# Expert layer: 49 of 128 hidden blocks made beside the choice of experts and the gates, 80 of 256 sums ranked, one-hot rows by wide comparisons

## The reference

```python
q = (h @ wq).reshape(B, S, PEER_HEADS, 2, PEER_QDIM // 2)
sub_scores = jnp.einsum('bshpk,hpnk->bshpn', q, subkeys)
top_v, top_i = lax.top_k(sub_scores, PEER_TOPK)                       # 16 of 128, twice for each of 8 heads
cand = (top_v[..., 0, :, None] + top_v[..., 1, None, :]).reshape(B, S, PEER_HEADS, 256)
cand_i = (top_i[..., 0, :, None] * N_KEYS + top_i[..., 1, None, :])
best_v, best_pos = lax.top_k(cand, PEER_TOPK)                         # 16 of 256 sums
expert = jnp.take_along_axis(cand_i, best_pos, axis=-1)
gates = jax.nn.softmax(best_v, axis=-1)
...
ub = jnp.take(u, eb, axis=0)
hid = jax.nn.gelu(jnp.einsum('tkd,td->tk', ub, xb)) * gb
vb = jnp.take(v, eb, axis=0)
return jnp.einsum('tk,tkd->td', hid, vb)
```

## Time and profile before

| | us |
|---|---|
| median of 3 runs | 3894.51 (3891.09 to 3894.8) |
| the profiled execution | 3889.89 |
| its span, first to last instruction | 3888.1 |
| DVE's last step of query to first keys | 590 to 628 |
| one-hot stage | 628 to 837 |
| start of dense | 837 to 864 |
| dense | 864 to 1922 |
| all that follows | 1922 to 3888 |

### The profile page before, as it was taken

How to read it: one execution, slowest core, us unless ns; L and a number is a source line. 1 busy time by engine, 2 the same in 40 slices (tenths; PEclk the granted TensorE clock), 3 DMA queues, 4 the chain that set the end, 5 groups by cost and what they waited for, 6 DMA issues and landing times.

```text
span 3888.1 us, 40982 instructions
## 1 busy us (share of the span) xinstructions
PE 3479.1 (89%) x16313; PEld 2824.5 (73%) x16313; DVE 2080.8 (54%) x3469; ACT 1499.7 (39%) x2428; POOL 766.2 (20%) x646
## 2 busy tenths in 40 slices
PE   5897993669999999999999997899898799899998
PEld 3466572659999999999878885678776474477887
DVE  2445599967666666666555524544532322344332
ACT  1222124965555555555532224345441111223222
POOL 0000104955444444444300000000000000000000
PEclk9895996879999999999989998999896598799999
DMA  4430511258777777777445522122121032032322
GB/s 170 131 114 1 201 49 44 125 209 303 278 277 278 273 274 274 274 281 280 142 152 184 185 81 82 68 82 68 58 91 37 0 102 83 6 98 83 96 98 76
DMA packets 175567, 554.74 MB, mean 143 GB/s; under 512 B 14801, under 2 KB 66385, under 8 KB 156945
## 3 DMA queue, kind: packets, MB, share of 16 engines
q1 hardware_dynamic: 138048, 350.52, 26.2%
q0 software_dynamic: 37328, 201.61, 14.5%
HBM read 514.06 MB, written 38.01 MB: 142 GB/s over the span
## 4 chain that ended last, share of the span: by engine, by line
PE 80%; DVE 14%; ACT 3%; DMA 2%; issue 1%; SPq 0%; DVEq 0%; ACTq 0%
PE ps L228 10%; PE ps L230 10%; PE ps L229 10%; PE ps L237 5%; PE ps L1329 4%; PE ps L1330 4%; PE ps L1315 4%; PE ps L1313 4%; PE ps L1314 4%; PE ps L1328 4%; DVE peerg_OH L1152 2%; PE ps L312 2%; PE ps L168 1%; PE ps L2033 1%; PE ps L2032 1%; PE ps L509 1%
## 5 line engine op out<-in xcount | busy, mean ns | idle before, releaser
L220 DVE TENSOR_TENSOR Wl<-W,Wh 128x1024 fp32r<-128x1024 f32 x363 | 438.1, 1207 | 716.1 <-ACT Wh L214 716.1
L214 ACT ACTIVATE Wh<-W 128x1024 fp32r<-128x1024 f32 x363 | 377.1, 1039 | 605.9 <-PE ps L230 570.0
L1292 POOL TENSOR_TENSOR peer_Y<-peer_Y,peerv_UV 128x1024 f32<-128x1024 f32 x128 | 380.2, 2970 | 531.6 <-ACT peerv_UV L1353 531.6
L1313 PE MATMUL ps<-peer_Hh,Wh 128*128 128x384 f32 x1024 | 344.8, 337 | 5.2 <-DVE Wl L220 5.2
L1315 PE MATMUL ps<-peer_Hh,Wl 128*128 128x384 f32 x1024 | 344.8, 337 | 0.0
L1314 PE MATMUL ps<-peer_Hl,Wh 128*128 128x384 f32 x1024 | 344.0, 336 | 0.0
L1330 PE MATMUL ps<-peerv_VH,peerv_HTl 128*128 128x512 f32 x768 | 301.4, 392 | 0.0
L1329 PE MATMUL ps<-peerv_VL,peerv_HTh 128*128 128x512 f32 x768 | 301.1, 392 | 0.0
L1328 PE MATMUL ps<-peerv_VH,peerv_HTh 128*128 128x512 f32 x768 | 298.9, 389 | 1.6 <-DVE peerv_HTl L1385 1.6
L1382 DVE TENSOR_TENSOR peerv_TG<-peerv_TG,peerv_GR 128x384 f32<-128x384 f32 x128 | 198.5, 1551 | 140.4 <-ACT peerv_TG L1358 140.4
L228 PE MATMUL ps<-f_Hh,Wh 128*128 128x512 f32 x672 | 262.3, 390 | 2.2 <-DVE Wl L220 2.2
(11 more groups left out here) (455 smaller groups left out, 6999.8 us busy)
## 6 DMA issues: line engine op xcount, KB each, us to landing
W<-peer_u SPq DMA_DIRECT2D x128, 512.0 KB, 7.2
peerv_VR<-peer_v SPq DMA_DIRECT2D x128, 512.0 KB, 3.6
gates_dram<-peerg_GB SPq DMA_DIRECT2D x12, 2048.0 KB, 6.6
peerv_GR<-gates_dram SPq DMA_DIRECT2D x32, 768.0 KB, 7.9
f_AW<-w_ada POOLq DMA_DIRECT2D x48, 512.0 KB, 4.3
W<-w_gate SPq DMA_DIRECT2D x44, 512.0 KB, 3.2
W<-w_up SPq DMA_DIRECT2D x44, 512.0 KB, 3.2
swa_AW<-w_ada POOLq DMA_DIRECT2D x32, 512.0 KB, 4.8
```

The costliest lines, as they stand in the source:

```text
L214: A.then_inc(e.activation(w_parts(i)[0], w_raw(i), ACT.Copy), ("w_hi", i))
L220: V.then_inc(e.tensor_tensor(lo, w_raw(i), hi.bitcast(F32), SUB), ("w", i))
L1292: G.then_inc(e.tensor_tensor(Y, Y, UV[:, k % NUV, 1024:2048], ADD), ("y", k))
L1313: e.matmul(o, hi[:, k, :], H2[0][:, k, 0:TD], start=k == 0, stop=False)
```

## The change

The hidden values (gelu of the products with u) don't depend on the choice. For 49 of the 128 blocks (`PRE`, spread over them with gaps of 2 and 3; the other 79 are `REST`) they are now made in gates: 12 while the choice of token block 0 runs, 32 one after every third q, and 5 behind the last q (`FIRST`, `BESIDE`). Each is 24 products into PSUM bank 5 or 6, a gelu to HS (ring of three), and a store to DRAM (`HID`) by SP. In dense these blocks need no u tile; SP loads the hidden rows (HI, ring of two) two blocks ahead, and the product with the gates and the split read them there.

Of the 256 sums 80 are made and ranked: row 0 with 16 columns, rows 1 to 7 with 8, rows 8 to 15 with the first. Three DVE operations make them for all heads, in place of eight; six small ones are added to turn a position into a row and a column. The result is the same choice.

One-hot A is one comparison of DVE (128 x 512, the keys and iota broadcast) for every q, multiplied by the gate on POOL (odd q, one operation) or on ACT (even q, four). One-hot B is the same on DVE (odd q) or four comparisons on POOL (even q). PSUM for the gates has five banks for six.

The copy of the last tokens (HK) and the zero of Y are made at the start of gates. v tiles 0 to 2 are loaded at its end. dense waits for the stores alone, no longer for all engines. Buffers are placed anew for this.

```diff
+    NC = 80
+    NOH, NHS = 5, 3
+    HS = P2.t("HS", NHS * TD, k=NHS)
+    HI = P3.t("HI", 2 * TD, k=2)
...
+    NPRE = 49
+    PRE = [2 + p * 126 // NPRE for p in range(NPRE)]
+    REST = [j for j in range(128) if j not in PRE]
+    t_u = t_pre + t_rest
+    NQ, FIRST = 96, 12
+    BESIDE = [("q", q) if k == "q" else ("h", FIRST + q // 3) for q in range(NQ) for k in ("qh" if q % 3 == 2 else "q")] \
+        + [("h", p) for p in range(FIRST + NQ // 3, NPRE)]
...
-        for h in range(8):
-            V.then_inc(e.tensor_tensor(CAND[:, h, :].rearrange("p (a b) -> p a b", a=16),
...
+        V.then_inc(e.tensor_tensor(CAND[:, :, 0:16], Va[:, :, 0:1].broadcast_to([128, 8, 16]), Vb, ADD))
+        V.then_inc(e.tensor_tensor(CAND[:, :, 16:72].rearrange("p h (a b) -> p h a b", b=8),
...
+        V.then_inc(e.tensor_tensor(CAND[:, :, 72:80], Va[:, :, 8:16], Vb[:, :, 0:1].broadcast_to([128, 8, 8]), ADD))
...
+    def keys_of(x, q):
+        return x[:, 4 * q:4 * q + 4].unsqueeze(2).broadcast_to([128, 4, 128])
...
+    def pre_pe(e, p):
+        if p >= 2:
+            A.wait_ge(e, ("pg", p - 2))
+        hidden_pe(e, ps(5 + p % 2)[:, 0:TD], t_pre[p], ("pa", p))
+    def pre_act(e, p):
+        PE.wait_ge(e, ("pa", p))
+        if p >= NHS:
+            hs_out[p % NHS].wait_ge(e, ("hs", p - NHS))
+        A.then_inc(e.activation(HS[:, p % NHS, :], ps(5 + p % 2)[:, 0:TD], ACT.Gelu), ("pg", p))
...
     def gates_dve(e):
+        w_lo(e, t_u[0])
+        ahead = best_dve(e, 0)
+        for p in range(FIRST):
+            w_lo(e, t_u[p + 1])
+            next(ahead, None)
+        run(ahead)
+        for kind, n in BESIDE:
+            if kind == "h":
+                w_lo(e, t_u[n + 1])
+                continue
...
+            oh_free(e, n)
+            V.then_inc(e.tensor_tensor(oh(n)[0], bc4(iota), keys_of(IT, n), EQ), ("oe", n))
+            if n % 2:
+                V.then_inc(e.tensor_tensor(oh(n)[1], bc4(iota), keys_of(JT, n), EQ), ("ob", n))
...
     def gates_pool(e):
+        G.then_inc(e.memset(Y, 0.0), ("y", -1))
+            if q % 2:
+                V.wait_ge(e, ("oe", q))
+                G.then_inc(e.tensor_tensor(OA, OA, keys_of(GT, q), MUL), ("oa", q))
+            else:
+                oh_free(e, q)
+                for s in range(4):
+                    ins = e.tensor_scalar(OB[:, s, :], iota, JT[:, c:c + 1], None, EQ)
...
     def gates_act(e):
+        for kind, n in BESIDE + [("q", NQ + i) for i in range(3)]:
+            if kind == "h":
+                pre_act(e, n - 1)
+                w_hi(e, t_u[n + 1])
+                continue
+            if n % 2 == 0 and n < NQ:
+                V.wait_ge(e, ("oe", n))
+                    ins = e.activation(oh(n)[0][:, s, :], oh(n)[0][:, s, :], ACT.Copy, scale=GT[:, c:c + 1])
+            if n >= 3:
+                p = n - 3
...
     def gates_pe(e):
+        hk_pe(e)
+        for p in range(FIRST):
+            if p == FIRST - 1:
+                run(picks)
+            pre_pe(e, p)
...
     def dense_act(e):
+            if j + 1 in rest_of:
+                w_hi(e, t_rest[rest_of[j + 1]])
...
     def dense_dve(e):
+            if j in pre_of:
+                hi_in[pre_of[j] % 2].wait_ge(e, ("hi", pre_of[j]))
+            else:
+                A.wait_ge(e, ("gelu", j))
+            x = rows_of(j)
```

## The result

The changed kernel took 3905.29 us (median of 9 runs, 3900.55 to 3913.44), the kernel before 3893.85 (9 runs, 3888.62 to 3895.51). The ratio is 1.0035, 95% interval 1.0024 to 1.0045: slower by about 11 us, just over the 0.2% that can be told from nothing. The forecast was 3871, faster; 3905 is inside the stated range and on the wrong side. The nearest case was rival 4, the gain given back entirely.

A forecast was written before the change was run, and what follows sets the result against it. DVE was taken to pace the one-hot stage of the kernel before, and PE, always busy, the dense stage. Costs of 19.5, 73 and 16 us less a gain of 131 made -23 us on the median: 3871 us, range 3812 to 3920.

The forecast's parts named there:

- rival 4: One-hot stage: queues run into each other, 100 to 104 us a third, gain given back entirely, 3895 us; chance 0.15.
- Dense stage: Dense stage: ACT, DVE and POOL chain, 7.71 or 6.57 us a step, 928 us for 1059.4, gain 131 us.
- Rival 3: Dense stage: PE's 6.71 us a block sets the pace instead of the chain, -65 us more, 3806 us; chance 0.06.
- First stretch: Before the one-hot stage: early u products delay the first keys to 647.3 us from 627.8, cost 19.5 us.
- One-hot stage: One-hot stage: POOL ends last at 94 us a third, 282 us for 209, cost 73 us.
- POOL's term: One-hot stage, a third: POOL's work 57 us undisturbed plus 37 lost beside DVE, sum 94 us.
- PE's term: One-hot stage, a third: PE needs 30 us for small products and 44.7 for u blocks, 75 us.
- Between the stages: From one-hot to dense stage: last u blocks, store and load put the first gates product at 970.5 us; 16 us new.
- The sum: Whole kernel: 19.5 + 73 + 16 - 131 = -23 us, last sum at 1898.5 for 1921.7, 3871 us.
- Rival 1: One-hot stage: POOL and DVE take turns for whole instructions, 110 us a third, 3919 us, slower; chance 0.17.
- Rival 2: One-hot stage: POOL's comparisons slip between DVE's; PE, DVE and ACT share the bound, 80 us a third, 3829 us; chance 0.22.

The follow-up runs named there:

- y_on_dve: Changed kernel with the row of Y scaled and added by VectorE in one operation, instead of ScalarE's scaling and GpSimd's addition: 3833.90 us, ratio 0.985.
- old_rows: Changed kernel with one-hot rows made one block at a time as in the kernel before, early u blocks and 80 sums kept: 3837.07 us, ratio 0.9866.

## Why the prediction was wrong, step by step

- **Dense stage, right.** 928 us were forecast with the chain of 7.71 and 6.57 a step; 928 were measured, the steps 7.70 and 6.57, the product with the gates 2.74 us at the median. Rival 3 (PE sets 6.71 a block) is out for this kernel, and is what y_on_dve then gave (856 us).
- **First stretch, right to 2 us, in part by luck.** First keys at 649.4, forecast 647.3. The first product of a u block came at 595.52 where 591.6 was forecast, since DVE came to its split 3.8 us later; the first block took 6.3 us and not 8.4, as the granted clock, 0.50 at first, rose within it.
- **One-hot stage, the step that failed.** "Sum 94 us. POOL ends last" took the stage's length from the fullest engine's sum. The terms, a third each, forecast against the middle third above: POOL 94 and 77, DVE 88 and 79 (with its waits for POOL), ACT at most 80 and 65, PE 75 and 85. All but PE's were too high, and the stage was still 105 and not 94. Two things were wrong that partly cancel. POOL's term was too large, and POOL, said to be over 95% busy, was at 75%: by the groups above a third is 64 x 0.893 + 16 x 1.309 = 78 us, 21 of losses over the undisturbed 57 where 37 had been given. And the length of the stage isn't the largest term where ACT and DVE each wait for the other's latest result. The prediction costed w_hi on ACT and w_lo on DVE and the scalings, but never wrote down in what order these stand in the two lists. The moved work adds two waits to a list that had none, and what is queued behind each is the other engine's next input. Turns as in the chain above, 8.3 to 14.7 us for each block of u, fill the 315 us. Moving one scaling out of every second turn gave back 18 of the 33 us that the forecast of the stage was short by. How the rest splits between the ring and POOL stays open.
- **PE's term.** 75 had 44.7 for the u blocks at full clock and 30 for the row products. The 30 took the 16 records of the earlier trace rows for four groups of tokens, but a group is 8 records (768 for the 96 groups), so they are two; and the 3.78 us were taken at a granted clock of 0.50. The two slips cancel: 16 such records take 2.05 us at full clock, 33 a third. In the changed kernel the granted clock was 0.89 to 0.92, and PE was busy 82 to 86 a third. It was not the bound.
- **Between the stages.** From the last product with rows, 963.8, to the first product with the gates, 1013.7, 50 us; 41 were forecast (929 to 970.5). Up to the issue of the last store of gates, at 989.1, it took 25 us where 27 were forecast; the rest took 24.6 for 14.5. The prediction let SP's stores of hidden rows go out beside the rest and ended with a load of gates. The chain of waits shows that SP issued three loads of v and then the last two stores of hidden rows, and that the gathers of u and v rows waited for those and took 10 us themselves:

```profile
989.44 0.43 SPq L1352
...
992.16 1.26 SPq L1210
...
993.46 8.10 DMA hidden_dram<-peerg_HS
...
1002.45 10.06 DMA peerv_UV<-peer_uv,peer_EX
```

  No run here took this store away, so its 8 us are read from the chain and not tested.
- **The sum.** The stage gave 315 for 282 (+33), the gap +9, the first keys +2, the dense stage 0: 44 us. By the times of the trace the last sum came at 1941.6 where 1898.5 was forecast, 43 later, and 20 later than the 1921.67 of the earlier trace rows. The profiled executions differ by 15 (3904.9 and 3889.9), since what follows that sum took 5 us less in this one; the medians differ by 11.
- **The rivals.** Rival 1 (whole instructions in turn, 110 us a third) came within 5 us of a third, but not for its reason: with GpSimd's products gone the stage was still 302. What it says of a single pair of operations is seen all the same, in the last section. Rival 2's 80 us a third is what old_rows reached (82) without the wide comparisons. Rival 4 named queues that run into each other at 100 to 104, and that comes nearest to what happened, though it didn't name ACT and DVE; it got 0.15, since I had no ring written down to price it by.

## What to carry to other kernels

When work moves into a stage, write the lists of the two engines that share it side by side and follow one turn round: if A's next input stands behind B's wait for A, the turn is the sum of both, however low each one's share is. A profile with every engine at 60 to 80% and two large waits pointing at each other is a sign of such a ring. First try another order, which needs no new instruction; but follow the new lists round as well, for the second order tried here made a ring of its own (ACT and PE). Before an operation is made wider to save instructions, see what it newly has to wait for and with whom it shares a port; and price a change that frees an engine together with the one that frees what lies right behind it.

## What the runs showed that was not expected

In the changed kernel four 128-wide comparisons of GpSimd took 3.06 or 8.74 us within 10 us of each other. VectorE's longest operations beside them were a reduction, with one input, in the first case, and comparisons, a split and products with two inputs in the second:

```profile
702.67 3.06 POOL L1247 TENSOR_SCALAR peerg_OH<-consts_sb,peert_JT 128x128 f32<-128x128 f32 x4
...
706.92 8.74 POOL L1247 TENSOR_SCALAR peerg_OH<-consts_sb,peert_JT 128x128 f32<-128x128 f32 x4
```

```profile
701.83 2.29 DVE L1132 TENSOR_REDUCE peerg_IJ<-peerg_EQ 128x128 f32<-128x2048 f32 x1
...
706.07 3.02 DVE L1125 TENSOR_TENSOR peerg_EQ<-peerg_PAB,consts_sb 128x2048 f32<-128x2048 f32 x1
709.22 1.23 DVE L220 TENSOR_TENSOR Wl<-W,Wh 128x1024 fp32r<-128x1024 f32 x1
...
712.38 2.29 DVE L1129 TENSOR_TENSOR peerg_EQ<-peerg_EQ,peerg_F 128x2048 f32<-128x2048 f32 x1
```

And one VectorE operation that scales and adds a 128x1024 row (1.28 us) replaced ScalarE's scaling of 1.16 us and GpSimd's addition of 2.40 to 3.15, while VectorE's own busy time fell: 128 x 1.28 = 164 us came in, and 128 x (2.74 - 0.555) = 280 us of waiting inside an operation went.
